# 644 rounded matrix products behind the last stage, read from shifted addresses

## The chip, the cores and the metric

The kernel runs on one core of one Trainium2 chip. The metric is the device time of one execution in microseconds (us). Before the change the median of 2 runs is 3341.47 us (3339.92 to 3343.01).

## The reference, cut to what matters

Two transformer stacks of depth 4 run one after the other on a sequence of 256 rows with 1024 features. The first has feed-forward and mixing layers, the second has four different mixers, each followed by an MLP. The program ends with the last MLP of the second stack:

```python
hm = _rms_norm(x, mlp_norm[i])
x = x + jnp.square(jax.nn.relu(hm @ mlp_w_up[i])) @ mlp_w_down[i]
```

Here `mlp_w_up` is 1024 x 4096 and `mlp_w_down` 4096 x 1024. What is returned is `x`, 256 x 1024 in float32. The change adds products whose results nothing reads, so the output is that of the kernel before.

## The kernel before, in words

All data is float32. The weights come in units of 128 x 1024 numbers (512 KB) through a ring of 8 slots, `ring`. ScalarE (L1438) rounds each unit into `ring_hi`, in the type fp32r. VectorE (L1977) writes what the rounding left off into `ring_lo`. The activations are split in the same way, into `act_hi` and `act_lo` for the input of a stage and `hid_hi` and `hid_lo` for the hidden layer. Each logical product is then three TensorE products of rounded operands: high by high, low by high and high by low.

In a product one operand is held in the array (it is loaded first, as a weight load, PEld in the profile) and the other is streamed past it, one column at a time. Two shapes make up nearly all of the work. In the rows the form `128x512` means 512 streamed columns, and `128x256` means 256.

- In the upward half of a feed-forward layer (`turned_half`, L897 to L899) 128 columns of a ring unit are held and 256 columns of `act_hi` or `act_lo` are streamed.
- In the downward half and in projections (`hi_products`, L796 and L797; `lo_product`, L800) 128 columns of activations are held and up to 512 columns of a ring unit are streamed.

Every tensor in these products starts at a multiple of 1024 bytes (`top` is rounded up to that at the start, and the tensors ahead of them have sizes that keep it). Slots, tiles and rows inside them are multiples of 1024 bytes too. So the streamed operand of every rounded product starts at a multiple of 1024 bytes. The held one starts there or 512 bytes past, since `wide = slice(col, col + P)` in `turned_half` and `ts = slice(t * P, (t + 1) * P)` elsewhere step by 128 numbers of 4 bytes.

Other products work on plain float32 operands, which are not rounded:

- transposes (`transposes`, L775), where the tile to be turned is held and a unit matrix is streamed;
- in one mixer, a convolution over 31 taps (`taps`, L1307), where the streamed operand is `conv_in[:, k, tap:tap + SEQ]` and so moves on by 4 bytes from tap to tap;
- in another mixer, transposes of heads that are 65 numbers wide, whose held tiles start 260 bytes apart.

Nothing schedules this program: each engine's instructions are in the order in which they are written. TensorE's stream ends with the last stage's `down` (its loops are written out, not looped over by the hardware). VectorE then adds the last sums to `x` (L2162), and SyncE sends `x` out in two halves (L686) and waits for both to land. The program is over when all engines have come to their end.

Of the kernel before, what the change touches and what calls it, by code (L numbers as in the profile page):

```python
# [14 lines left out]
P = 128  # L15
SEQ = 256
# [4 lines left out]
HALF = 512  # L21
RING = 8
# [111 lines left out]
def build(nc, a, out, stages):  # L134
    with ExitStack() as ctx:
# [7 lines left out]
        def sb(name, shape, dt=F32, over=None, skip=0):  # L143

            size = int(np.prod(shape[1:])) * 4
            if over is None:
                at = top[0]
                top[0] += -(-size // 32) * 32
            else:
                at = where[over] + skip  # L150
            where[name] = at
            return nc.alloc_sbuf_tensor_at(name + "_sb", shape, dt, offset=at)
# [4 lines left out]
        ring_hi = sb("ring_hi", [P, RING, 2, HALF], F32R)  # L157
# [4 lines left out]
        act_hi = sb("act_hi", [P, KT, SEQ], F32R)  # L162
        act_lo = sb("act_lo", [P, KT, SEQ], F32R)
        hid_hi = sb("hid_hi", [P, 32, SEQ], F32R)
# [77 lines left out]
        def C(name):  # L242
            for t, w in ((con, WHERE), (con_1, WHERE_1), (con_2, WHERE_2)):
                if name in w:
                    at, n = w[name]
                    return t[:, at:at + n]

        ident = C("ident")
        upto, from_on, ones = C("upto"), C("from_on"), C("ones")
# [10 lines left out]
        T = [ctx.enter_context(nc.psum_tensor(f"T{b}", [P, HALF], F32)) for b in range(2)]  # L260
# [166 lines left out]
        def early_out(kind):  # L427
            return sum(what == "out" and TT - 1 in ts for what, _, ts, *_ in DEAL[kind])
# [28 lines left out]
        def widths_of(kind):  # L457
            if kind in FUSED_CHUNKS:
                return [sum(w for _, w in pieces) for pieces in FUSED_CHUNKS[kind]]
            return [w for _, w in chunks_of(2 * MEMW if kind == "mem_kv" else WIDTH[kind])]  # L460
# [300 lines left out]
        def _(pe):  # L761
            c = Counts()
            mm = nc.tensor.matmul
# [93 lines left out]
            def linear(lhs, width, start=2, after={}):  # L857

                n, g = c["unit"], c["g"]
                full = width // HALF  # L860
                widths = [w for _, w in chunks_of(width)]
                if start:
                    opening(n, g)
                pairs = (full - start) // 2
                if pairs > 1:
                    with pe.Fori(0, pairs) as i:
                        for d in (start, start + 1):
                            chunk(lhs, d % 2, HALF, n + d * CHUNK_UNITS, g + max(d - 1, 0) + 2 * i, RING, i)
                for d in range(start + (2 * pairs if pairs > 1 else 0), len(widths)):
                    chunk(lhs, d % 2, widths[d], n + d * CHUNK_UNITS, g + max(d - 1, 0))  # L870
                    if d in after:
                        after[d]()
                c["unit"] = n + len(widths) * CHUNK_UNITS
                c["g"] = g + len(widths)
# [522 lines left out]
            for kind, *arg in stages:  # L1397
                if kind == "mem_kv":
                    pe.wait_ge(memn_ready, c.up("memn"))
                    linear(MEM_PAIR, 2 * MEMW, start=0)  # L1400
                elif kind == "ffn":
                    up_down(FF1 // SEQ, True, FF1 // P)
                elif kind == "mlp":
                    up_down(FF2 // HALF, False, FF2 // P)
                elif kind in FUSED_CHUNKS:
                    fused(kind)
                elif kind == "conv":
                    conv()


        @block.scalar
# [1519 lines left out]
```

## Time and profile before

| what | value |
|---|---|
| median of 2 runs | 3341.47 us |
| the profiled execution's own time | 3342.41 us |
| its span, first to last instruction | 3340.7 us |
| TensorE busy | 3218.8 us, 96% of the span |
| mean granted TensorE clock | 0.991 of full speed |
| VectorE, ScalarE, GpSimd busy | 58%, 49%, 4% |

The span runs from the first to the last instruction of the program on the core. The execution's own time is 1.7 us longer than the span. A TensorE row gives the start of a product and a duration that includes its way through the array, so two products in a row overlap in the profile; what a product costs in a dense stretch is the distance from its start to the next one's.

### The profile page before, as it was taken

What the parts mean: (1) busy time and instruction counts of PE and PEld (TensorE: products, weight loads), DVE (VectorE), ACT (ScalarE), POOL (GpSimd) and SP (SyncE); (2) the same over time, 40 slices, a digit from 0 to 9 for tenths busy, and PEclk for the clock granted to TensorE, in tenths of its full rate; (3) what the DMA queues carried; (4) which work ended last, traced back from release to release, by engine and by line L of the source; (5) the groups of instructions that cost most, each with busy time, mean ns of one, the idle gap of its engine ahead of it and who ended that gap; (6) DMA issues with size and microseconds to landing.
All of it is one profiled execution on the core that took longest, in us unless ns stands there. A gap on an engine that the chain in (4) does not pass through costs nothing.

```text
span 3340.7 us, 52167 instructions
## 1 busy us (share of the span) xinstructions
PE 3218.8 (96%) x19661; PEld 2857.0 (86%) x19661; DVE 1950.2 (58%) x2911; ACT 1627.7 (49%) x2426; POOL 142.8 (4%) x230
## 2 busy tenths in 40 slices
PE   7999999999999999999999999999999999999999
PEld 7977988977898977897987897879788988987797
DVE  4566546655555554655556656565566558655663
ACT  4445444445444445544445444555354446545552
POOL 1010000000000000000000101000000000001000
PEclk9999999999999999999999999999999999999999
DMA  6654656552555543465654554425544550555364
GB/s 214 190 183 128 201 176 192 180 164 89 170 182 186 185 158 114 157 187 171 196 190 158 177 181 158 147 99 184 168 160 137 189 184 32 195 189 164 109 204 154
DMA packets 413280, 551.71 MB, mean 165 GB/s; under 512 B 33952, under 2 KB 263520, under 8 KB 413104
## 3 DMA queue, kind: packets, MB, share of 16 engines
q1 hardware_dynamic: 409248, 536.10, 49.7%
q0 software_dynamic: 2864, 10.38, 0.9%
q10 hardware_dynamic: 992, 2.84, 0.2%
q8 instruction: 115, 1.88, 0.2%
q14 instruction: 61, 0.50, 0.0%
HBM read 548.15 MB, written 1.05 MB: 164 GB/s over the span
## 4 chain that ended last, share of the span: by engine, by line
PE 87%; DVE 8%; ACT 3%; issue 1%; DMA 1%; POOL 0%; ACTq 0%; DVEq 0%; SPq 0%
PE G L796 15%; PE G L800 15%; PE G L797 15%; PE G L897 11%; PE G L899 11%; PE G L898 11%; DVE ring_lo_sb L1977 3%; PE T L775 2%; PE S L1000 1%; PE O L1028 1%; DVE act_hi_sb L1991 1%; ACT ring_hi_sb L1438 1%; DVE act_lo_sb L2001 1%; PE G L1307 0%; PE G L1051 0%
## 5 line engine op out<-in xcount | busy, mean ns | idle before, releaser
L1977 DVE TENSOR_TENSOR ring_lo_sb<-ring_sb,ring_hi_sb 128x1024 fp32r<-128x1024 f32 (+1 forms) x1028 | 1219.7, 1208 | 585.0 <-ACT ring_hi_sb L1438 566.9
L1438 ACT ACTIVATE ring_hi_sb<-ring_sb 128x1024 fp32r<-128x1024 f32 (+1 forms) x1028 | 1054.9, 1043 | 643.8 <-DMA ring_sb<-ffn_w_down 206.5
L897 PE MATMUL G<-act_hi_sb,ring_hi_sb 128*128 128x256 f32 x3136 | 890.6, 284 | 3.1 <-DVE ring_lo_sb L1977 3.1
L899 PE MATMUL G<-act_hi_sb,ring_lo_sb 128*128 128x256 f32 x3136 | 888.1, 283 | 0.0
L898 PE MATMUL G<-act_lo_sb,ring_hi_sb 128*128 128x256 f32 x3136 | 888.0, 283 | 0.0
L897 PEld LDWEIGHTS G<-act_hi_sb,ring_hi_sb 128*128 128x128 f32 x3136 | 602.6, 192 | 3.4 <-issue 3.4
L898 PEld LDWEIGHTS G<-act_lo_sb,ring_hi_sb 128*128 128x128 f32 x3136 | 602.6, 192 | 0.0
L899 PEld LDWEIGHTS G<-act_hi_sb,ring_lo_sb 128*128 128x128 f32 x3136 | 602.5, 192 | 0.0
L796 PE MATMUL G<-ring_hi_sb,hid_hi_sb 128*128 128x512 f32 x1456 | 573.6, 394 | 10.0 <-DVE hid_hi_sb L2010 6.6
L797 PE MATMUL G<-ring_lo_sb,hid_hi_sb 128*128 128x512 f32 x1456 | 569.4, 391 | 0.0
L800 PE MATMUL G<-ring_hi_sb,hid_lo_sb 128*128 128x512 f32 x1248 | 485.5, 389 | 0.0
L796 PE MATMUL G<-ring_hi_sb,act_hi_sb 128*128 128x512 f32 (+2 forms) x960 | 384.6, 401 | 36.5 <-DVE ring_lo_sb L1977 22.6
L797 PE MATMUL G<-ring_lo_sb,act_hi_sb 128*128 128x512 f32 (+2 forms) x960 | 369.6, 385 | 0.0
L2050 DVE TENSOR_TENSOR work_sb<-G,work_sb 128x256 f32<-128x256 f32 (+1 forms) x240 | 117.0, 492 | 396.6 <-ACT work_sb L1489 396.6
L796 PEld LDWEIGHTS G<-ring_hi_sb,hid_hi_sb 128*128 128x128 f32 x1456 | 275.0, 189 | 68.4 <-DVE hid_hi_sb L2010 8.4
L800 PE MATMUL G<-ring_hi_sb,act_lo_sb 128*128 128x512 f32 (+2 forms) x960 | 324.0, 382 | 7.3 <-DVE act_lo_sb L2001 7.3
L797 PEld LDWEIGHTS G<-ring_lo_sb,hid_hi_sb 128*128 128x128 f32 x1456 | 275.0, 189 | 55.5
L1489 ACT ACTIVATE work_sb<-G 128x256 f32<-128x256 f32 (+1 forms) x120 | 52.7, 439 | 538.8 <-PE G L899 444.7
L800 PEld LDWEIGHTS G<-ring_hi_sb,hid_lo_sb 128*128 128x128 f32 x1248 | 234.3, 188 | 49.0
L796 PEld LDWEIGHTS G<-ring_hi_sb,act_hi_sb 128*128 128x128 f32 x960 | 185.0, 193 | 95.8 <-DVE ring_lo_sb L1977 35.6
L800 PEld LDWEIGHTS G<-ring_hi_sb,act_lo_sb 128*128 128x128 f32 x960 | 181.4, 190 | 46.1 <-issue 12.2
L797 PEld LDWEIGHTS G<-ring_lo_sb,act_hi_sb 128*128 128x128 f32 x960 | 185.4, 193 | 31.1
(274 smaller groups left out, 2555.1 us busy)
## 6 DMA issues: line engine op xcount, KB each, us to landing
ring_sb<-ffn_w_gate_up SPq DMA_DIRECT2D x704, 256.0 KB, 3.9
ring_sb<-ffn_w_down SPq DMA_DIRECT2D x352, 256.0 KB, 3.7
ring_sb<-mlp_w_up SPq DMA_DIRECT2D x256, 256.0 KB, 3.7
ring_sb<-mlp_w_down SPq DMA_DIRECT2D x256, 256.0 KB, 3.7
ring_sb<-a_w_in SPq DMA_DIRECT2D x48, 256.0 KB, 4.8
ring_sb<-sb_w_in SPq DMA_DIRECT2D x48, 256.0 KB, 3.9
ring_sb<-moba_w_in SPq DMA_DIRECT2D x48, 256.0 KB, 4.1
ring_sb<-w_mem_kv SPq DMA_DIRECT2D x32, 256.0 KB, 3.6
```

The lines of the kernel that those rows point to most:

```text
L775: last = nc.tensor.transpose(bank[0:m, at:at + P], src, ident)
L796: mm(dst, lhs[0][:, kt, ts], ring_hi[:, slot, k, 0:w], start=start, stop=False)
L797: mm(dst, lhs[0][:, kt, ts], ring_lo[:, slot, k, 0:w], start=False, stop=False)
L800: return mm(dst, lhs[1][:, kt, ts], ring_hi[:, slot, k, 0:w], start=False, stop=stop)
L897: mm(dst, hi, act_hi[:, kt, :], start=(kt == 0 and f == 0), stop=False, skip_group_check=True)
L898: mm(dst, hi, act_lo[:, kt, :], start=False, stop=False, skip_group_check=True)
L899: last = mm(dst, lo, act_hi[:, kt, :], start=False, stop=(kt == KT - 1), skip_group_check=True)
L1000: last = mm(S[:, t, 0:w], q, keys, start=(t == 0), stop=True, skip_group_check=True)
L1438: fn(ring_hi[:, s_, :, 0:w], ring[:, s_, :, 0:w], ACT.Copy).then_inc(hi_ready, 1)
L1489: fn(gated[:, par, 1, 0:w], G[:, 1, par, 0:w], f).then_inc(gated_ready, 1)
L1977: v.tensor_tensor(ring_lo[:, s_, :, 0:w], ring[:, s_, :, 0:w], ring_hi[:, s_, :, 0:w], ALU.subtract).then_inc(lo_ready, 1)
L2050: v.tensor_tensor(hid[:, par, t, 0:w], G[:, t, par, lo:lo + w], gated[:, par, t, 0:w], ALU.mult).then_inc(g_taken[t], 1)
```

## The change

TensorE gets a function `offsets`, called once behind the last stage. It holds 45 groups. A group is 12 or 16 rounded products into one PSUM bank (`T[0]`), each written over or added to the same 512 or 256 columns, and behind them one transpose of a float32 table (`from_on`) into the same bank. Nothing waits for these instructions, they wait for no semaphore, and no other engine's stream changes.

```diff
@@ -1407,6 +1407,33 @@
                 elif kind == "conv":
                     conv()
 
+            def offsets():
+
+                def block_of(n_mm, lhs, rhs):
+                    for j in range(n_mm):
+                        m = rhs(j)
+                        mm(T[0][:, 0:m.shape[1]], lhs(j), m, start=(j == 0), stop=True, skip_group_check=True)
+                    nc.tensor.transpose(T[0][:, 0:P], from_on, ident)
+
+                a_flat = act_hi[:, :, :].rearrange("p k n -> p (k n)")
+                h_flat = hid_hi[:, :, :].rearrange("p k n -> p (k n)")
+
+                def acts(off=0):
+                    return lambda j: a_flat[:, 2 * P * (j % 6) + off:2 * P * (j % 6) + off + P]
+
+                def units(off, n):
+                    return lambda j: ring_hi[:, j % RING, :, :].rearrange("p k n -> p (k n)")[:, off:off + n]
+
+                def rows(off):
+                    return lambda j: h_flat[:, SEQ * j + off:SEQ * j + off + SEQ]
+                for off in (*range(0, 256, 16), 4, 8, 12):
+                    block_of(12, acts(), units(off, HALF))
+                for off in (*range(0, 256, 16), 4, 8, 12):
+                    block_of(16, units(0, P), rows(off))
+                for off in range(16, 128, 16):
+                    block_of(16, units(off, P), rows(0))
+            offsets()
+
```

`off` counts numbers of 4 bytes. So there are three kinds of groups:

| kind | groups | products in each | held | streamed | offset in bytes |
|---|---|---|---|---|---|
| 1 | 19 | 12 | `act_hi`, 128 columns, offset 0 | `ring_hi`, 512 columns | 0, 64, ... 960, and 16, 32, 48 |
| 2 | 19 | 16 | `ring_hi`, 128 columns, offset 0 | `hid_hi`, 256 columns | 0, 64, ... 960, and 16, 32, 48 |
| 3 | 7 | 16 | `ring_hi`, 128 columns | `hid_hi`, 256 columns, offset 0 | 64, 128, ... 448 for the held one |

That makes 228 products that stream 512 columns and 416 that stream 256. The streamed operand is off a multiple of 1024 bytes in 18 of the 19 groups of kind 1 (216 products) and 18 of kind 2 (288 products), and the held one in the 112 products of kind 3.

The order of TensorE's instructions at the end of its stream, where the first rows are the last two products of the last stage and the rows with a plus are new (the names are output, then streamed and held operand; `con_sb` holds the tables, and L1415 and L1416 are the two lines of `block_of`):

```order
 L797 MATMUL G<-ring_lo_sb,hid_hi_sb 128x512
 L800 MATMUL G<-ring_hi_sb,hid_lo_sb 128x512
+L1415 MATMUL T<-ring_hi_sb,act_hi_sb 128x512 x12
+L1416 MATMUL T<-con_sb 128x128
+L1415 MATMUL T<-ring_hi_sb,act_hi_sb 128x512 x12
+L1416 MATMUL T<-con_sb 128x128
```

Nothing stands between the last product of the stage and the first new one. The second place is where the groups of kind 1 end and those of kind 2 begin, in the same stream:

```order
+L1415 MATMUL T<-ring_hi_sb,act_hi_sb 128x512 x12
+L1416 MATMUL T<-con_sb 128x128
+L1415 MATMUL T<-hid_hi_sb,ring_hi_sb 128x256 x16
+L1416 MATMUL T<-con_sb 128x128
+L1415 MATMUL T<-hid_hi_sb,ring_hi_sb 128x256 x16
+L1416 MATMUL T<-con_sb 128x128
```

Here `hid_hi` becomes the streamed operand and `ring_hi` the held one. All 45 groups stand in one row like this, and the program's end follows.

## Rows read from the trace of the kernel before

**Rows 1.** The page's span, TensorE's busy share, and its clock in 40 slices.

```profile
span 3340.7 us, 52167 instructions
PE 3218.8 (96%) x19661; PEld 2857.0 (86%) x19661; DVE 1950.2 (58%) x2911; ACT 1627.7 (49%) x2426; POOL 142.8 (4%) x230
PE   7999999999999999999999999999999999999999
PEclk9999999999999999999999999999999999999999
```

**Rows 2.** Timeline of all engines, 3336.0 to 3341 us: start, duration, engine, line.

```profile
start us, us, engine line op out<-in xcount [idle before <-releaser]
3335.79 0.39 PE L797 MATMUL G<-ring_lo_sb,hid_hi_sb 128*128 128x512 f32 x1
3336.02 0.39 PE L800 MATMUL G<-ring_hi_sb,hid_lo_sb 128*128 128x512 f32 x1
3336.45 1.22 DVE L2162 TENSOR_TENSOR x_sb<-G,x_sb 128x1024 f32<-128x1024 f32 x1 [6.93 <-PE G L800]
3337.70 0.34 SPq L686 DMA_DIRECT2D out<-x_sb  x1
```

**Rows 3.** Busy time of two dense stretches: length, each engine's busy time (instructions), PEclk.

```profile
3200.00:3240.00 40.00, 40.00 (x336) 40.00 (x335) 22.29 (x23) 20.19 (x24) 0.00 (x0) 1.00 0.61 197
3300.00:3330.00 30.00, 30.00 (x134) 24.86 (x133) 12.25 (x10) 9.55 (x9) 0.00 (x0) 1.00 0.38 129
```

**Rows 4.** Timeline of TensorE, 512 streamed columns, last stage.

```profile
3295.22 0.39 PE L800 MATMUL G<-ring_hi_sb,hid_lo_sb 128*128 128x512 f32 x1
...
3296.58 0.39 PE L800 MATMUL G<-ring_hi_sb,hid_lo_sb 128*128 128x512 f32 x1
```

**Rows 5.** Timeline of TensorE, 256 streamed columns, last stage.

```profile
3203.82 0.28 PE L897 MATMUL G<-act_hi_sb,ring_hi_sb 128*128 128x256 f32 x1
...
3205.50 0.28 PE L899 MATMUL G<-act_hi_sb,ring_lo_sb 128*128 128x256 f32 x1
```

**Rows 6.** Timeline of TensorE: transposes between products of 512 streamed columns.

```profile
1831.13 0.40 PE L800 MATMUL G<-ring_hi_sb,hid_hi_sb 128*128 128x512 f32 x1
1831.36 0.60 PE L775 MATMUL T<-con_sb,nrm_sb 128*128 128x128 f32 x4
1831.72 0.48 PE L796 MATMUL G<-ring_hi_sb,hid_hi_sb 128*128 128x512 f32 x1
1832.04 0.39 PE L797 MATMUL G<-ring_lo_sb,hid_hi_sb 128*128 128x512 f32 x1
```

**Rows 7.** Timeline of TensorE: transposes between products of 256 streamed columns.

```profile
2745.23 0.28 PE L899 MATMUL G<-act_hi_sb,ring_lo_sb 128*128 128x256 f32 x1
2745.35 0.60 PE L775 MATMUL T<-con_sb,work_sb 128*128 128x128 f32 x4
2745.71 0.36 PE L897 MATMUL G<-act_hi_sb,ring_hi_sb 128*128 128x256 f32 x1
2745.91 0.28 PE L898 MATMUL G<-act_lo_sb,ring_hi_sb 128*128 128x256 f32 x1
```

**Rows 8.** All transposes of `work` tiles: durations in ns, minimum, median, maximum.

```profile
L775 PE MATMUL T<-con_sb,work_sb x344: 270/272/474, 43.1 to 3191.5; 128*128 128x128 f32 x172
```

**Rows 9.** Timeline of TensorE: plain float32, streamed operand moving on 4 bytes per tap.

```profile
2772.24 7.15 PE L1307 MATMUL O<-conv_in_sb,more_diags_sb 128*128 128x256 f32 x32
```

**Rows 10.** Durations of these products, minimum, median, maximum ns, by output.

```profile
L1307 PE MATMUL S<-conv_in_sb,diags_sb x42: 377/378/381, 2763.1 to 2771.9; 128*128 128x256 f32 x42
```

**Rows 11.** Timeline of TensorE: transposes of heads 65 numbers wide (held).

```profile
1305.96 0.60 PE L775 MATMUL T<-con_sb,proj_sb 128*65 128x128 f32 x4
```

**Rows 12.** Busy time of two stretches in which the granted clock was halved (columns as rows 3).

```profile
48.00:51.00 3.00, 3.00 (x16) 3.00 (x15) 3.00 (x5) 3.00 (x6) 2.20 (x5) 0.50 1.07 368
2206.00:2211.00 5.00, 5.00 (x12) 3.94 (x13) 3.50 (x3) 1.96 (x3) 0.00 (x0) 0.50 0.00 0
```

**Rows 13.** Timeline of TensorE in these two stretches, first and last row of each.

```profile
48.22 0.42 PE L898 MATMUL G<-act_lo_sb,ring_hi_sb 128*128 128x256 f32 x1
...
50.78 0.41 PE L898 MATMUL G<-act_lo_sb,ring_hi_sb 128*128 128x256 f32 x1
2206.92 0.63 PE L800 MATMUL G<-ring_hi_sb,hid_hi_sb 128*128 128x512 f32 x1
...
2210.76 0.63 PE L800 MATMUL G<-ring_hi_sb,hid_hi_sb 128*128 128x512 f32 x1
```

## The prediction

> **What bounds the kernel now.** I read the page first: TensorE is busy for 96% of the span, at a clock that is nearly always full [rows 1]. Then I read the timeline at the end, because the change stands there. The last product starts at 3336.02 us and ends at 3336.41. VectorE adds the last half to `x` from 3336.45 on, and the output transfer, issued at 3337.70, takes the rest of the 3340.7 us [rows 2]. So 4.3 us of the span lie behind TensorE's last instruction. Only they can cover what is added, as TensorE has no other idle time there: in the last 30 us stretch it is busy throughout, with 134 products [rows 3].
>
> **What a product costs.** The distance between starts is the price, not the printed duration.
>
> - 512 streamed columns: six distances from 3295.22 to 3296.58 us, 1.36 / 6 = 0.227 us [rows 4]. The count agrees: 30 us with 134 products that touch the stretch gives 0.224 to 0.226 [rows 3].
> - 256 streamed columns: fourteen distances from 3203.82 to 3205.50, 1.68 / 14 = 0.120 us [rows 5]. In this stretch the held operand lies alternately 0 and 512 bytes past a multiple of 1024, and the price doesn't change with it.
> - A transpose among them: from the last product to the first transpose 0.23 us (512 columns) or 0.12 (256), so a product costs the same before it. Four transposes then take 1831.72 - 1831.36 = 0.36 us until the next product starts. Durations of 0.27 us [rows 8] inside a row of 0.60 make three distances of 0.11, so the last transpose is followed after 0.36 - 0.33 = 0.03 us. The product behind it needs 0.32 us until its successor instead of 0.227 (512 columns) [rows 6], and 0.20 instead of 0.120 (256 columns) [rows 7]. One transpose thus costs 0.03 + 0.09 = 0.12 us, or 0.03 + 0.08 = 0.11. No row shows a single transpose between products; I take the end of a row of four for it, as the nearest. If the full 0.11 of an inner one came on top, it would be 45 x 0.08 = 3.6 us more.
>
> **The sum with no effect of the offset.** It removes nothing and moves nothing; it adds.
>
> - Kind 1: 12 x 0.227 + 0.12 = 2.84 us a group, times 19 = 54.0 us.
> - Kinds 2 and 3: 16 x 0.120 + 0.11 = 2.03 us a group, times 26 = 52.8 us.
> - Together 106.8 us. The first new product starts 0.23 us behind the last old one, at 3336.25. The 106.8 us count up to where a product after the last transpose would start, 0.03 us behind it; so the last transpose starts at 3443.0 and ends 0.27 later, at 3443.3.
> - The output transfer is still issued at about 3337.7 and lands under this. VectorE, SyncE and the other engines get nothing and wait for nothing new; nothing is queued behind the new products but TensorE's own end. The end of the execution moves from the transfer to TensorE: 3443.3 - 3340.7 = 102.6 us more.
> - The profiled execution took 3342.41 us, so 3445.0 with the same 1.7 us around the span. The median of the runs is 0.9 us below the profiled execution. I forecast **3444 us**.
>
> **The unknown: what an offset costs.** No rounded product of the kernel before streams from an address off 1024 bytes, so this is bounded from both sides by the nearest rows. The nearest in kind are the convolution's taps. They stream plain float32 numbers from addresses that move on by 4 bytes per tap, and 32 records of them take 7.15 us in one row. Without the last one's 0.38 that is 6.77 / 31 = 0.218 us each [rows 9], and their durations stay within 377 to 381 ns over every offset [rows 10]. So a start at an arbitrary multiple of 4 bytes costs nothing, or at most some 4 ns. The held side has a case too: four transposes of heads that lie 260 bytes apart take 0.60 us, the same as four with aligned tiles [rows 11, 6, 7]. Hence my value of zero.
>
> What speaks against it: these plain records take 0.218 us for 256 columns, where a rounded product takes 0.120. The plain stream runs at about half the pace, and a penalty could hide in that slack. So the upper bound is that the fast stream works only from aligned starts and otherwise falls to half pace. That pace also stands in the stretches with a clock of 1.2 GHz, where the granted clock is 0.50 [rows 12]: 2.56 / 12 = 0.213 us for 256 columns and 3.84 / 9 = 0.427 for 512 [rows 13]. The lower bound is below zero. At 1.2 GHz the prices are the plain stream's, 0.213 and 0.427; at 2.4 GHz they should be half of that, 0.107 and 0.213, but they are 0.120 and 0.227. Some 13 ns of each rounded product are thus no streaming, and a cause that lies in how the two operands' addresses fall would let an offset take them away.
>
> The Trainium skill, "TensorE: Matmul & The Clock Gate", section "Back-to-back issue gap", gives N / 2.4 + 2.5 ns at full clock; the rows are some 11 ns above it. By this rule alone the sum would be 228 x 0.216 + 416 x 0.109 plus the transposes, an estimate of about 7 us less.
>
> **The rivals.**
>
> 1. *Half pace off alignment, at every offset.* For it: the slack above. Against it: the f32 taps run alike at all offsets, and rounded operands are still 4-byte numbers. Price: 216 x (0.427 - 0.227) = 43.2, and 288 x (0.213 - 0.120) = 26.8, together 70 us: **3514 us**. Chance 6%. The Trainium skill, "SBUF — State Buffer", section "A bandwidth-pool intuition that's wrong (but worth ruling out)", gives a moving operand about 614 GB/s, as 128 lanes x 2 bytes x 2.4 GHz. For numbers of 4 bytes that is half pace, an estimate of 0.427 us for 512 columns; the aligned 0.227 already breaks that rule, so it could hold only off alignment, which is this rival.
> 2. *Half pace only at 16, 32 and 48 bytes* (the 64-byte multiples are all alike). Price: 3 groups of 12 x 0.200 = 7.2, and 3 of 16 x 0.093 = 4.5: **3456 us**. Chance 8%. For it: a memory may be read in lines longer than 16 bytes. The taps speak against it as above.
> 3. *A small toll per product off alignment*, or a dearer weight load for kind 3. A toll of 4 ns, the taps' scatter, is 504 x 0.004 = 2 us; a toll of 13 ns, as much as the present surplus, is 6.6. The held one: 112 x 0.05 = 5.6 if a load came out of its cover. **3446 to 3452 us**. Chance 9%.
> 4. *The surplus of 13 ns goes away off alignment*: 616 products x 0.013 = 8 us less, **3436 us**. Chance 4%.
> 5. *Not slower: the added work isn't counted.* If the execution were over when the output has landed, the 102.6 us behind it would lie outside the measure and the time would stay at **3341 us**. It decides by whether the end waits for all engines. For it: nothing reads the new products. Against it: TensorE's stream must run to its end, and the execution's time has only 1.7 us outside the span. Chance 2%. (A change below 2%, 67 us, is about what a measurement can't tell; the sum is clear of it by 36 us.)
> 6. *The clock is halved in the groups*, as it was in the stretches of rows 12. It would add up to 228 x 0.200 + 416 x 0.093 = 84 us, **3528 us**. TensorE has worked without a pause for over 100 us there and goes on without one, so 1%.
>
> The forecast, no effect, keeps 70%.
>
> **How the numbers follow.** Around 3444 the known terms are uncertain by 3 to 4 us: the single transposes up to +3.6, and the prices' rounding (0.0005 us x 644) and the runs' spread of 1.5 either way. Rivals 3 and 2 lie above this, up to 3456, and I take them in; rival 4 lies just below. The range is **3437 to 3458**, which leaves out rivals 1, 4, 5 and 6, 13 in 100 together. Slower by over 2% has 98%, within 2% has 2% (rival 5), and faster has none, as no row offers a way to it.
>
> **What would show each step.** In the profile after, the last old product still starts near 3336.0, the output transfer is issued near 3337.7, and TensorE goes on to about 3443. Starts lie 0.227 us apart in kind 1 and 0.120 in kinds 2 and 3, in all groups, the first with offset 0 and those behind it alike. Another distance in all but the first group of a kind is rival 1, 3 or 4; in the last three alone it is rival 2. A pause at each transpose beyond 0.12 us shows that term too small. A span that still ends near 3340.7 would prove my reading of the end wrong.

## The result and the profile after

The changed kernel takes 3441.39 us (median of 2 runs, 3440.95 to 3441.83), against 3341.47 us before: a ratio of 1.0299, with an interval of 1.0255 to 1.0343. The forecast was 3444 us, and the time lies in its range of 3437 to 3458.

The page after, where it answers to [rows 1]:

```profile
span 3439.2 us, 53545 instructions
PE 3322.3 (97%) x20350; PEld 2951.1 (86%) x20350; DVE 1949.3 (57%) x2911; ACT 1628.7 (47%) x2426; POOL 146.7 (4%) x230
PEclk9999999999999999999999999999999999999999
```

TensorE has 689 products more, 644 and 45 transposes, and 103.5 us more busy time. VectorE and ScalarE have the instructions that they had, and their busy time within 1 us.

The timeline of all engines where the new part begins, and where it ends (start and duration in us; it answers to [rows 2]; L2189 is what L2162 was, 27 lines further down):

```profile
3331.90 0.39 PE L800 MATMUL G<-ring_hi_sb,hid_lo_sb 128*128 128x512 f32 x1
3332.12 2.89 PE L1415 MATMUL T<-ring_hi_sb,act_hi_sb 128*128 128x512 f32 x12
3332.32 1.23 DVE L2189 TENSOR_TENSOR x_sb<-G,x_sb 128x1024 f32<-128x1024 f32 x1 [6.94 <-PE G L800]
3333.58 0.34 SPq L686 DMA_DIRECT2D out<-x_sb  x1
3334.85 0.27 PE L1416 MATMUL T<-con_sb 128*128 128x128 f32 x1
...
3438.70 0.28 PE L1416 MATMUL T<-con_sb 128*128 128x128 f32 x1
```

The first group starts 0.23 us behind the last old product. The output transfer is issued while it runs. The last transpose ends at 3438.98 us, and the new part has taken 3438.98 - 3332.12 = 106.9 us. The forecast had 3443.3 - 3336.25 = 107.05.

The stages ahead, which the change does not touch, ended 4.1 us earlier than in the profile before (3331.90 against 3336.02). The profiled execution took 3440.95 us, where 3445.0 was forecast for it, and these 4.1 us are that difference.

Busy time of the whole new part, its kind 1 and then its kinds 2 and 3 (columns as in [rows 3]):

```profile
3332.00:3386.80 54.80, 54.80 (x248) 44.03 (x247) 1.23 (x1) 0.00 (x0) 0.00 (x0) 1.00 0.03 10
3386.90:3439.00 52.10, 52.08 (x444) 51.84 (x442) 0.00 (x0) 0.00 (x0) 0.00 (x0) 1.00 0.00 1
```

The granted clock is 1.00 in both. Behind the last addition to `x` and the output transfer, the other engines and the DMA stand still.

Inside the new part the groups are not alike. The timeline of TensorE, two neighbours of kind 1 (the streamed operand 448 bytes and 512 bytes past a multiple of 1024), then two of kind 2 with the same offsets:

```profile
3352.18 3.05 PE L1415 MATMUL T<-ring_hi_sb,act_hi_sb 128*128 128x512 f32 x12
3355.07 0.27 PE L1416 MATMUL T<-con_sb 128*128 128x128 f32 x1
3355.10 3.00 PE L1415 MATMUL T<-ring_hi_sb,act_hi_sb 128*128 128x512 f32 x12
3357.93 0.27 PE L1416 MATMUL T<-con_sb 128*128 128x128 f32 x1
...
3400.85 2.08 PE L1415 MATMUL T<-hid_hi_sb,ring_hi_sb 128*128 128x256 f32 x16
3402.77 0.27 PE L1416 MATMUL T<-con_sb 128*128 128x128 f32 x1
3402.79 2.16 PE L1415 MATMUL T<-hid_hi_sb,ring_hi_sb 128*128 128x256 f32 x16
3404.79 0.27 PE L1416 MATMUL T<-con_sb 128*128 128x128 f32 x1
```

The price of a group is the distance from its first product to the next group's. At 448 bytes it is 2.92 us (512 columns) and 1.94 us (256 columns). At 512 bytes it is 2.86 (3357.96, the next start, less 3355.10) and 2.03 (3404.82 - 3402.79). So an offset does count, with opposite signs in the two shapes. The distance below is that of the two operands' starts, streamed minus held, modulo 256 bytes; in kinds 1 and 2 it is the offset modulo 256, as the held operand stays at a multiple of 1024. The group prices over the new part are read from the trace in ns (rows shown are rounded to 0.01 us, so a difference of two can be 0.01 us off):

| distance, bytes | kind 1, 12 x 512 columns, us | kind 2, 16 x 256 columns, us |
|---|---|---|
| 0 | 2.75 (the first of all), 2.87, 2.86, 2.86 | 2.02, 2.03, 2.03, 2.03 |
| 64 | 2.87, 2.86, 2.88, 2.88 | 1.93, 2.00, 2.00, 2.00 |
| 128 | 2.90, 2.89, 2.89, 2.89 | 2.03, 2.01, 2.00, 2.01 |
| 192 | 2.92, 2.92, 2.92, 2.92 | 1.95, 1.94, 1.94, 1.94 |

From the second value on the rows repeat every 256 bytes, within 0.02 us. At 16, 32 and 48 bytes kind 1 takes 2.89, 2.92 and 2.90 us, and kind 2 takes 2.02, 1.99 and 2.01. In kind 3, with the held operand 64, 128, ... 384 bytes up, it is 1.95, 2.01, 2.00, 2.02, 2.00 and 2.02. The starts in a dense group of kind 2 are 120 ns apart at distance 0, 118 at 64 and 113 at 192.

### The profile page after: what moved, and what is told of

The parts are those of the page before. It is cut to its first block, busy times and chain, and to the rows that moved or that the text cites. A ratio compares the mean times of both kernels' runs of the same rounds, so it can differ in the third digit from the quotient of the medians.

```text
span 3439.2 us, 53545 instructions
## 1 busy us (share of the span) xinstructions
PE 3322.3 (97%) x20350; PEld 2951.1 (86%) x20350; DVE 1949.3 (57%) x2911; ACT 1628.7 (47%) x2426; POOL 146.7 (4%) x230
## 3 DMA queue, kind: packets, MB, share of 16 engines
q10 hardware_dynamic: 992, 2.84, 0.2%
## 4 chain that ended last, share of the span: by engine, by line
PE 87%; DVE 8%; ACT 3%; issue 1%; DMA 0%; POOL 0%; SPq 0%; DVEq 0%; ACTq 0%
PE G L796 15%; PE G L800 14%; PE G L797 14%; PE G L897 11%; PE G L898 11%; PE G L899 11%; DVE ring_lo_sb L2004 3%; PE T L1415 3%; PE T L775 2%; PE S L1000 1%; PE O L1028 1%; DVE act_hi_sb L2018 1%; ACT ring_hi_sb L1465 1%; DVE act_lo_sb L2028 1%; PE G L1307 0%
## 5 line engine op out<-in xcount | busy, mean ns | idle before, releaser
L897 PE MATMUL G<-act_hi_sb,ring_hi_sb 128*128 128x256 f32 x3136 | 890.6, 284 | 3.2 <-DVE ring_lo_sb L2004 3.2
L898 PE MATMUL G<-act_lo_sb,ring_hi_sb 128*128 128x256 f32 x3136 | 888.1, 283 | 0.0
L899 PE MATMUL G<-act_hi_sb,ring_lo_sb 128*128 128x256 f32 x3136 | 888.0, 283 | 0.0
L897 PEld LDWEIGHTS G<-act_hi_sb,ring_hi_sb 128*128 128x128 f32 x3136 | 602.5, 192 | 3.4 <-issue 3.4
L898 PEld LDWEIGHTS G<-act_lo_sb,ring_hi_sb 128*128 128x128 f32 x3136 | 602.6, 192 | 0.0
L899 PEld LDWEIGHTS G<-act_hi_sb,ring_lo_sb 128*128 128x128 f32 x3136 | 602.5, 192 | 0.0
L1516 ACT ACTIVATE work_sb<-G 128x256 f32<-128x256 f32 (+1 forms) x120 | 52.8, 440 | 541.6 <-PE G L899 447.6
```

The lines of the kernel that those rows point to most:

```text
L897: mm(dst, hi, act_hi[:, kt, :], start=(kt == 0 and f == 0), stop=False, skip_group_check=True)
L898: mm(dst, hi, act_lo[:, kt, :], start=False, stop=False, skip_group_check=True)
L899: last = mm(dst, lo, act_hi[:, kt, :], start=False, stop=(kt == KT - 1), skip_group_check=True)
L1516: fn(gated[:, par, 1, 0:w], G[:, 1, par, 0:w], f).then_inc(gated_ready, 1)
```

## The experiments

Where a number of the new part is given, it is read from the run's trace, from the first new product's start to the end of the last one.

**The changed kernel again.**

> The changed kernel once more, unaltered. In its first profile the last old product started 4.1 us earlier than in the kernel before, and the sum of the new part was 107.1 us as forecast. Theory A (the stages ahead scatter by some us from run to run, and the new part costs 107 us behind them): the difference of the medians comes out between 99 and 104 us, and the stages' part of the profile differs again by up to 5 us either way. Theory B (the added code itself makes the stages ahead faster by 4 us): the last old product starts near 3332 us again and the difference stays near 98 to 100 us.

It took 3443.26 us against 3339.68 us before, a ratio of 1.0312 (1.0294 to 1.0329), so 103.6 us more. The last old product started at 3332.8 us, and the new part took 106.9 us, group by group the same as in the first run within 2 ns (the expectation calls it 107.1; both traces give 106.9). Over all runs with added products the last old product started at 3330.3, 3331.8, 3331.9, 3332.8, 3335.1, 3336.6 and 3337.9 us. That scatter of 7.6 us holds the 3336.0 of the kernel before. The medians' difference fits theory A. This repeat alone could not have ruled out B, as the interval of its difference is 98 to 110 us and its stages ended at 3332.8, near B's 3332. The runs below in which they ended at 3336.6 and 3337.9, with the added code in place, do rule it out.

**All offsets 0.**

```diff
-                    block_of(12, acts(), units(off, HALF))
+                    block_of(12, acts(), units(0, HALF))
-                    block_of(16, units(0, P), rows(off))
+                    block_of(16, units(0, P), rows(0))
-                    block_of(16, units(off, P), rows(0))
+                    block_of(16, units(0, P), rows(0))
```

> All 45 groups with offset 0, the number of products unchanged. Theory A (an offset costs or saves a few ns a product, by its rest modulo 256 bytes): every group of 512 columns takes 2.84 us (first profile: 2.86 to 2.92 with an offset), every group of 256 columns 2.02 us (1.93 to 2.03 with one), so the new part becomes 106.3 us, 0.9 us less for kind 1 and 0.8 us more for kinds 2 and 3 against the changed kernel; the total is the same within 1.5 us. Theory B (the few ns are left from position in the stream or from phase, not from the offset): the groups scatter as before although all offsets are 0.

It took 3444.01 us, a ratio of 1.0310 (1.0293 to 1.0328), the same as with offsets. The new part took 107.3 us, 0.4 more than with offsets. Kind 1 became 0.35 us cheaper (54.41 against 54.76), kinds 2 and 3 0.76 dearer. Groups of 256 columns are now alike. The timeline of TensorE shows three of them:

```profile
3393.29 2.16 PE L1415 MATMUL T<-hid_hi_sb,ring_hi_sb 128*128 128x256 f32 x16
...
3395.31 2.16 PE L1415 MATMUL T<-hid_hi_sb,ring_hi_sb 128*128 128x256 f32 x16
...
3397.33 2.16 PE L1415 MATMUL T<-hid_hi_sb,ring_hi_sb 128*128 128x256 f32 x16
```

They start 2.02 us apart. All groups of kinds 2 and 3 take 2.02 to 2.03, and none has the 1.94 of distance 192. So the pattern belongs to the offset, and theory B is out. One point of theory A missed: kind 1 does not fall to 2.84 us at offset 0 but alternates between 2.86 and 2.88, so some 0.03 us a group above the forecast's 2.84 do not come from the offset. In the trace the products behind each transpose stand 224 to 236 ns apart, and half of the groups then settle at 226.7.

**No transposes.**

```diff
-                    nc.tensor.transpose(T[0][:, 0:P], from_on, ident)
```

> The 45 transposes are left out, the 644 products stay. Theory A (a single transpose costs 0.11 to 0.12 us, 0.03 behind it and 0.09 at the next product): the new part is 5.2 us shorter. Theory B (a single one costs a full transpose more, 0.2 us): 9 us shorter. Theory C (the transposes reset a phase between held and streamed operand, and this sets the pattern of 113 to 120 ns): without them the groups of one offset no longer repeat their pattern.

```profile
3337.94 0.39 PE L800 MATMUL G<-ring_hi_sb,hid_lo_sb 128*128 128x512 f32 x1
3338.17 52.87 PE L1415 MATMUL T<-ring_hi_sb,act_hi_sb 128*128 128x512 f32 x228
3390.87 49.10 PE L1415 MATMUL T<-hid_hi_sb,ring_hi_sb 128*128 128x256 f32 x416
```

In this timeline of TensorE the products stand in two unbroken rows, and the new part ends at 3390.87 + 49.10 = 3439.97 us. It has taken 101.8 us, 5.05 less than in the changed kernel, which makes 0.112 us a transpose: the end of a row of four was the right row to price it from, and theory B is out. The measured time, 3441.85 us (a ratio of 1.0306, 1.0289 to 1.0323), is only 1.4 us below the repeat. The two profiled executions show how such a term goes unseen: their spans are 3440.2 and 3440.1 us, as the stages ahead ended 5.2 us later in this one. The total can't tell a term of 5 us here, the trace can. Without transposes the groups of one distance still repeat their pattern, so theory C is out as well. One thing does change: the first group at 64 bytes now runs at 118 ns like its successors, and no longer at 113.

**Steps of 4 bytes.**

```diff
-                for off in (*range(0, 256, 16), 4, 8, 12):
+                for off in range(19):
-                for off in (*range(0, 256, 16), 4, 8, 12):
+                for off in range(19):
-                for off in range(16, 128, 16):
+                for off in range(1, 8):
```

> The offsets step by 4 bytes instead of 64: 0, 4, ... 72 bytes for the streamed operand in kinds 1 and 2, and 4 to 28 bytes for the held one in kind 3. Theory A (as the plain float32 taps: any multiple of 4 bytes within a few ns): the new part stays between 105 and 110 us. Theory B (a line of 16 bytes must be read twice when a start is off 16 bytes): the groups off a multiple of 16 bytes are dearer, up to half pace, 0.427 and 0.213 us a product; 14 groups of each kind then cost 14 x 12 x 0.2 = 34 us and 14 x 16 x 0.093 = 21 us more.

It took 3442.95 us (1.0313, 1.0296 to 1.0330), and the new part 107.8 us. The timeline of TensorE at 4, 8 and 12 bytes, kind 1:

```profile
3334.78 3.09 PE L1415 MATMUL T<-ring_hi_sb,act_hi_sb 128*128 128x512 f32 x12
3337.70 0.27 PE L1416 MATMUL T<-con_sb 128*128 128x128 f32 x1
3337.73 3.04 PE L1415 MATMUL T<-ring_hi_sb,act_hi_sb 128*128 128x512 f32 x12
...
3340.64 3.00 PE L1415 MATMUL T<-ring_hi_sb,act_hi_sb 128*128 128x512 f32 x12
3343.47 0.27 PE L1416 MATMUL T<-con_sb 128*128 128x128 f32 x1
```

The group 4 bytes off takes 2.95 us, 7 ns a product more than at 0. Over all 19 offsets kind 1 lies between 2.84 and 2.95 us (the first group aside) and kind 2 between 1.98 and 2.08. The new part lies in theory A's range, though single groups of kind 1 differ by up to 9 ns a product. Nothing comes near half pace, so theory B is out. The Trainium skill, "SBUF — State Buffer", section "Specifications (TRN2)", states cachelines of 16 bytes and a penalty for each cross to a new line. The trace has some toll at 4 bytes, but at 12 bytes, which is off a 16-byte line too, kind 1 takes 2.86 us as at 0; such lines alone do not give this order.

**Both operands shifted by the same offset.**

```diff
-                    block_of(12, acts(), units(off, HALF))
+                    block_of(12, acts(off), units(off, HALF))
-                    block_of(16, units(0, P), rows(off))
+                    block_of(16, units(off, P), rows(off))
-                    block_of(16, units(off, P), rows(0))
+                    block_of(16, units(off, P), rows(off))
```

> The held and the streamed operand are shifted by the same offset in all three kinds (16 to 960 bytes, 0 to 448 bytes in kind 3), so their distance modulo 256 bytes stays 0. Theory R (only the distance of the two addresses modulo 256 bytes decides): all groups at 64-byte multiples behave as with offset 0, 2.86 to 2.88 us for 512 columns and 2.02 to 2.03 us for 256, and none shows distances of 113 ns. Theory S (the streamed address alone decides): groups of kind 2 at 192 bytes past a multiple of 256 take 1.94 us and those of kind 1 there 2.92 us, as in the changed kernel.

It was run once and took 3439.64 us; what it shows is in the trace, where the new part took 107.1 us. The timeline of TensorE at 448 and 512 bytes for both operands, kind 2:

```profile
3398.99 2.16 PE L1415 MATMUL T<-hid_hi_sb,ring_hi_sb 128*128 128x256 f32 x16
3400.99 0.27 PE L1416 MATMUL T<-con_sb 128*128 128x128 f32 x1
3401.02 2.16 PE L1415 MATMUL T<-hid_hi_sb,ring_hi_sb 128*128 128x256 f32 x16
```

This group took 1.94 us where only the streamed operand was shifted; now it takes 2.02. At multiples of 64 bytes all groups of kinds 2 and 3 take 2.02 to 2.03, and those of kind 1 2.85 to 2.87, theory R's values within 0.01. So at these offsets the streamed address alone decides nothing: what counts is the distance between the two operands' starts, modulo 256 bytes. The held side in the changed kernel says the same: its group at 64 bytes, which is the distance 192 seen from the streamed side, took 1.95 us. The one at 320 bytes is at distance 192 too and took 2.00, with its products 117 to 119 ns apart, the pace of distance 64. The kernels below show this second pace again. At 16, 32 and 48 bytes for both operands kind 2 takes 1.98, 2.03 and 2.00 us, where distance 0 gives 2.02 to 2.03 elsewhere, so off the multiples of 64 the distance alone does not fix the price.

**The distance put into the kernel before.** The 9408 products of L897 to L899 have 256 streamed columns and distance 0, the dear case. In three kernels without any added product `act_hi` and `act_lo` were moved 192, 64 or 256 bytes up, by placing small tensors ahead of and behind them. For 192:

```diff
+        gates = sb("gates", [P, TT, 3 * H2])
         act_hi = sb("act_hi", [P, KT, SEQ], F32R)
         act_lo = sb("act_lo", [P, KT, SEQ], F32R)
+        small = sb("small", [P, 64])
+        sums = sb("sums", [P, 64])
+        den = sb("den", [P, 64])
+        pool_tmp = sb("pool_tmp", [P, 16])
...
```

> The kernel before, without the added products, with act_hi and act_lo placed 192 bytes past a multiple of 1024 (small tensors are moved around them, all other tensors of rounded products stay where they were). The 9408 products of L897 to L899 then stream from an address 192 bytes past that of the held operand modulo 256. Theory R, if it carries over from the added groups: their distance falls from 120 to 113.3 ns, 9408 x 6.7 ns = 63 us, the 384 of the fused mixers give 2.6 more, and the 2880 that hold act tiles cost 0.4 ns more each, 1 us: 3275 to 3280 us. If something else takes over as the limit (the ring's transfers, ScalarE or VectorE), less of it comes out. Theory N (the pattern belongs to the groups alone, with their fixed order of slots): the same 3340 us.

> As act192, with a distance of 64 bytes. Theory R: products of L897 to L899 at 117.8 ns (9792 x 2.2 = 21.5 us less), but the 2880 that hold act tiles are at the dear distance of kind 1, 4 ns more each (11.5 us): some 10 us less, 3330 us. If the first pattern of kind 2 at 64 bytes (113 ns) takes hold instead, up to 50 us less. Theory N: 3340 us.

> As act192, with a distance of 256 bytes. Theory R (modulo 256): products at 120 ns and 3340 us, no change. If act192 gains and this one gains as well, the cause is not the distance modulo 256 but the moved small tensors or the loss of the 1024-byte start.

| distance | time, us | ratio to before (3341.99 us) | mean distance of starts, L897 / L898 / L899, ns |
|---|---|---|---|
| 0 (the kernel before) | 3341.99 | 1 | 121.0 / 120.1 / 120.1 |
| 192 | 3286.63 | 0.9833 (0.9819 to 0.9846) | 115.5 / 114.5 / 114.3 |
| 64 | 3324.62 | 0.9950 (0.9934 to 0.9965) | 118.8 / 117.7 / 117.8 |
| 256 | 3340.95 | 0.9997 (0.9987 to 1.0006) | 120.9 / 120.1 / 120.1 |

The interval at 192 lies clear of 1. The timeline of TensorE at distance 192, in the stretch that answers to [rows 5], and its busy time over 30 us (columns as in [rows 3]), then the same 30 us view at 256:

```profile
3149.73 0.28 PE L898 MATMUL G<-act_lo_sb,ring_hi_sb 128*128 128x256 f32 x1
...
3151.88 0.28 PE L899 MATMUL G<-act_hi_sb,ring_lo_sb 128*128 128x256 f32 x1
```

```profile
3150.00:3180.00 30.00, 30.00 (x268) 30.00 (x267) 21.36 (x21) 17.89 (x21) 0.00 (x0) 1.00 0.56 187
```

```profile
3200.00:3230.00 30.00, 30.00 (x252) 30.00 (x251) 20.69 (x21) 17.31 (x20) 0.00 (x0) 1.00 0.52 174
```

The two rows at 192 are 19 products apart: 2.15 / 19 = 0.113 us, against 0.120 in [rows 5]. In 30 us TensorE now touches 268 products instead of 252, at the same clock. The gain is 55.4 us, where 60 to 65 were expected. The starts account for it: the three lines save 5.5, 5.6 and 5.8 ns each, times 3136 = 53 us. Why the mean is not the 6.7 ns of the groups shows in the same trace. Its busy time in two other dense stretches, both at distance 192:

```profile
1070.00:1100.00 30.00, 30.00 (x257) 30.00 (x256) 18.15 (x20) 15.92 (x21) 0.00 (x0) 1.00 0.61 186
1400.00:1430.00 30.00, 30.00 (x267) 30.00 (x266) 17.20 (x19) 13.99 (x18) 0.00 (x0) 1.00 0.61 185
```

The products of L897 to L899 stand in 31 unbroken stretches of 48 to 768. In 22 of them they settle at 113.3 ns, and in 9, with 2016 products, at 117.8 ns from end to end. These 2016 products miss 4.5 ns each, 9 us of the 63. So a distance of 192 bytes allows two paces; what picks one of them was not found. The kernel at 64 bytes moves the same five small tensors as this one and gains a third as much. The control at 256 bytes moves four small tensors, has its operands off 1024 bytes as well, and gains nothing. So it is the distance modulo 256.

At 64 bytes the gain is 17.4 us (12 to 22 by the interval), 10 expected. The two terms are there: L897 to L899 save 2.2 to 2.4 ns each, 22 us, in all 31 stretches at 117.8 ns, and the 512-column products with held activations settle at some 233.3 ns instead of 228.3, 12 us for 2544 of them. In the profiled execution the sum of the distances at all products with held activations grows by 5.7 us only, waits included, so the waits among them became shorter. By the traces the gain is thus 22 - 6 = 16 us.

**A finer look at the distance.**

```diff
-                for off in (*range(0, 256, 16), 4, 8, 12):
+                for off in range(0, 66, 2):
-                for off in (*range(0, 256, 16), 4, 8, 12):
+                for off in range(0, 66, 2):
-                for off in range(16, 128, 16):
-                    block_of(16, units(off, P), rows(0))
```

> A finer look at the distance of streamed and held operand: 33 groups of kind 1 and 33 of kind 2, the streamed offset going from 0 to 256 bytes in steps of 8. The new part holds 396 products of 512 columns and 528 of 256. Theory A (192 bytes is the bottom of a broad trough for 256 columns): the groups from 176 to 208 bytes take 1.94 us, the others 1.98 to 2.08, and kind 1 is dearest in the same place, 2.92 us. Theory B (the dependence has no smooth course; the cheap and the dear places are single values where held and streamed reads fall into step): neighbours 8 bytes apart differ as much as any two. In either case the new part takes 33 x 2.88 + 33 x 2.01 = 161 us within 2 us.

It was run once and took 3499.98 us, beside one run of the kernel before at 3345.93; what it shows is in the trace. The timeline of TensorE, kind 1 at 40 bytes, then kind 2 at 184, 192 and 200 bytes:

```profile
3349.71 3.12 PE L1415 MATMUL T<-ring_hi_sb,act_hi_sb 128*128 128x512 f32 x12
...
3352.70 0.48 PE L1415 MATMUL T<-ring_hi_sb,act_hi_sb 128*128 128x512 f32 x1
...
3477.55 2.17 PE L1415 MATMUL T<-hid_hi_sb,ring_hi_sb 128*128 128x256 f32 x16
3479.59 2.08 PE L1415 MATMUL T<-hid_hi_sb,ring_hi_sb 128*128 128x256 f32 x16
3481.53 2.17 PE L1415 MATMUL T<-hid_hi_sb,ring_hi_sb 128*128 128x256 f32 x16
3483.56 0.36 PE L1415 MATMUL T<-hid_hi_sb,ring_hi_sb 128*128 128x256 f32 x1
```

At 184 bytes the group takes 2.03 us, at 192 1.94, at 200 2.03. There is no trough; 192 is a single place, and the next cheapest of the 33 are 112 bytes (1.98) and 32, 144, 160 and 240 bytes (1.99). The dearest of kind 2 is 232 bytes, 2.08. Kind 1 is dearest at 40 bytes, 2.99 us with its products exactly 240 ns apart, and cheapest at 104 bytes, 2.87, with 64, 80 and 256 bytes at 2.88 (the first group aside). The new part took 162.7 us, at the upper edge of what was expected. Theory A is out. Theory B holds in that the course is not smooth: neighbours 8 bytes apart differ by up to 0.09 us in kind 2, where all 33 lie within 0.14. Its reason, reads that fall into step, is not shown by this.

## Why the prediction was right, point by point

- **TensorE is what ends the program.** Right: nothing of the 106.9 us is hidden but what had lain behind the last product. The end moved to TensorE, and rivals 5 (not counted) and 6 (halved clock) did not come, the latter as the granted clock of 1.00 in the new part shows.
- **The prices.** Right in the sum, where two small errors cancel. Kind 1 was forecast at 54.0 us and took 54.8; kinds 2 and 3 were forecast at 52.8 and took 51.8, both counted to where a next product would start. Of the 0.8 over in kind 1, 0.35 is offset, by the kernel with all offsets 0, and the rest stands there too. Of the 1.0 under in kinds 2 and 3, 0.76 is offset by the same kernel. The check by count was read a little low: a product that began up to 0.39 us ahead touches the stretch too [rows 3], so it gives 30.39 / 134 = 0.227 us, the price itself. In the traces products of 512 columns settle at 226.7 ns. The Trainium skill, "TensorE: Matmul & The Clock Gate", section "Back-to-back issue gap", gives the formula that the prediction quotes, N / 2.4 + 2.5 ns, for a product by itself, and for a stream of loads and products some 131 ns at 512 columns. The traces agree with neither.
- **A single transpose: 0.11 to 0.12 us.** Right, 0.112 by leaving them out.
- **An offset costs nothing.** This step was wrong, though its sum was right. In the runs an offset changes a product by -6.7 to +13 ns at full clock; in the changed kernel the signs of the two shapes cancel to -0.4 us. That they cancel was luck: no row of the prediction held the two signs. Two rows had misled me. The held operand at 0 and 512 bytes [rows 5] is the same distance modulo 256 bytes, so it could not show a difference. And the plain float32 taps [rows 9, 10] stream at half the pace and show at most 4 ns, as the prediction's text had feared.
- **The surplus of 13 ns.** Rival 4 had it that the surplus lies in how the two addresses fall and may go away off alignment. It gave 4 in 100 to that for all shapes. It is half true for one shape at one distance: 256 columns at 192 bytes keep 7 of the 13 ns. Rival 3, a toll of 4 ns, is borne out for 512 columns at 192 bytes, and at 4 bytes it is 7 ns. Rivals 1 and 2, half pace, are out.
- **The forecast against the measured time.** Of the 4.05 us between the profiled execution and its forecast, the stages ahead are 4.1, and they scatter by 7.6 us over the repeats. Against medians of 4 and 7 runs, 103.6 us more, the forecast of 102.6 is 1.0 us short. The prediction put the spread of the runs at 1.5 us either way, from two runs. Fifteen later runs of the kernel before lie between 3339.02 and 3345.20, so this term was too small, and that the forecast came within 2.6 us of the median was partly luck.

What stays open is the mechanism. At multiples of 64 bytes the distance decides which paces can come. The effect is there at full clock and not bound to DMA or other engines (they stand still in nearly all of the new part), and a group's price repeats to 2 ns in the repeat of the changed kernel. Which of two paces a stretch takes at distances 64 and 192, and which part of the chip makes the surplus, was not separated.

## What to carry to other kernels

In a dense stretch of rounded float32 products, read the distance between starts against columns / 2.4 GHz, and if there is a surplus, try the two operands' starts at several distances modulo 256 bytes: it costs a few bytes of SBUF. At 256 columns a distance of 192 bytes between held and streamed operand made the kernel before 1.7% faster, 3286.63 us, a ratio of 0.9833, although not every stretch took the better pace. The distance has to be tried for each shape, as 512 columns are dearer at the same 192 bytes (2.92 us a group against 2.86). When using a row as evidence that something makes no difference, ask first whether the row could have shown one; and a sum that comes out right doesn't vouch for its zero terms.

## What the runs showed of the hardware that was not expected

- At full clock, where starts settle on one distance, it is mostly 113.3, 117.8 or 120 ns (256 columns) and 226.7, 233.3 or 240 ns (512 columns). But for 117.8 these are multiples of 6.67 ns, 16 columns at 2.4 GHz, above the bare 106.7 and 213.3 ns of the two shapes (half of the 0.213 and 0.427 us at 1.2 GHz [rows 13]). At other distances, 128 bytes for one, they repeat a pattern of 115 to 122 ns instead.
- The settled pattern takes some products to come up. With all offsets 0, a group of 256 columns runs at 116 to 121 ns for five or seven products behind the first and then at 120.
- One distance can have two paces. Kind 2 at 64 bytes took 1.93 us once (113.3 ns) and then 2.00 (117.8 ns), in both runs of the changed kernel alike. At 192 bytes a whole stretch of 768 products ran at 117.8 ns, and others of the same length at 113.3.
